# Low parts of the weights in one GpSimd subtraction each, with a wait for its end

## The reference

```
for l in range(2):
    h = rms_norm(x); z = h @ w_in            # one wide projection, split in 17 parts
    hm = mlstm(silu(conv(q, k)), v, gates)   # chunks of 128 tokens, 4 heads
    ha = dsa_attention(...)                  # 8 index heads, the 64 best keys, 8 heads
    hr = retention(rotary(rq), rotary(rk), rv)
    y = sig(g_m) * (hm @ p_m) + sig(g_a) * (ha @ p_a) + sig(g_r) * (hr @ p_r)
    x = x + y @ w_out
    x = x + (silu(h2 @ w_gate) * (h2 @ w_up)) @ w_down      # D_FF = 2816
x = rms_norm(x)
```

## Time and profile before

| | |
|---|---|
| median of 3 runs | 1605.23 us (1604.74 to 1609.58) |
| profiled execution | 1606.26 us |
| its span | 1604.4 us |
| mean granted clock of TensorE | 0.985 of full speed |
| PE busy | 1528.0 us, 95% |
| POOL busy | 1228.4 us, 77% |
| ACT busy | 714.5 us, 45% |
| DVE busy | 689.3 us, 43% |
| front (layer 0, layer 1, second block up to the experts) | 0 to about 1200 us |
| feed-forward network of layer 1 | about 782 to 960 us |

### The profile page before, as it was taken

One profiled execution on the slowest core, in us unless ns is written; L12 is line 12 of the kernel. 1 busy time (PEld: TensorE's weight loads), 2 busy tenths in 40 slices (PEclk: granted clock), 3 DMA queues, 4 the chain that ended last, 5 costly groups with the idle time before them and its releaser, 6 DMA issues.

```text
span 1604.4 us, 21618 instructions
## 1 busy us (share of the span) xinstructions
PE 1528.0 (95%) x7018; PEld 1163.9 (73%) x7018; DVE 689.3 (43%) x1306; ACT 714.5 (45%) x879; POOL 1228.4 (77%) x1185
## 2 busy tenths in 40 slices
PE   7989989999999999999999999999999899999986
PEld 5767867788887777877788887878785656646534
DVE  3995854310017977844301027456534122122215
ACT  4544543544446544543544445546341422315323
POOL 7997897988889997888888899978591633639713
PEclk9999999999999999999999999999999999999998
DMA  6754444677765553455677665645363989899990
GB/s 221 216 175 126 130 146 132 205 217 215 226 201 171 158 153 121 125 153 144 190 220 219 189 189 186 184 140 178 92 200 143 363 328 344 344 389 395 398 361 34
DMA packets 95526, 333.84 MB, mean 208 GB/s; under 512 B 11136, under 2 KB 15760, under 8 KB 94384
## 3 DMA queue, kind: packets, MB, share of 16 engines
q1 hardware_dynamic: 88240, 307.26, 58.3%
q10 hardware_dynamic: 6048, 21.22, 4.4%
q0 software_dynamic: 1152, 4.19, 0.7%
HBM read 322.12 MB, written 21.00 MB: 214 GB/s over the span
## 4 chain that ended last, share of the span: by engine, by line
POOL 49%; PE 27%; issue 19%; DMA 2%; DVE 1%; ACT 1%; POOLq 1%; ACTq 0%; DVEq 0%; SPq 0%
POOL w_lo L1890 48%; PE bank L1211 5%; PE bank L692 4%; PE bank L1279 3%; PE bank L1229 3%; PE bank L1248 3%; PE bank L696 2%; PE bank L1302 2%; PE bank L1342 1%; DMA arena<-in_experts 1%; DMA logits<-outputs_by_expert,tiny 1%; POOL w_lo L1905 1%; ACT w_hi L1455 1%; POOLq L1885 1%; PE bank L1111 0%
## 5 line engine op out<-in xcount | busy, mean ns | idle before, releaser
L1890 POOL TENSOR_TENSOR w_lo<-raw,w_hi 128x256 fp32r<-128x256 f32 (+1 forms) x1092 | 1034.2, 981 | 163.2 <-ACT w_hi L1455 161.6
L1455 ACT ACTIVATE w_hi<-raw 128x1024 fp32r<-128x1024 f32 x371 | 392.6, 1059 | 530.4 <-PE bank L696 274.9
L692 PE MATMUL bank<-w_hi,hT 128*128 128x512 f32 x2240 | 599.5, 400 | 22.3 <-DVE hT L2006 7.1
L692 PEld LDWEIGHTS bank<-w_hi,hT 128*128 128x128 f32 x2240 | 419.5, 191 | 118.2 <-issue 14.0
L696 PE MATMUL bank<-w_lo,hT 128*128 128x512 f32 x1120 | 328.1, 395 | 10.8 <-POOL w_lo L1890 10.8
L696 PEld LDWEIGHTS bank<-w_lo,hT 128*128 128x128 f32 x1120 | 211.4, 190 | 62.1 <-POOL w_lo L1890 17.1
L1905 POOL TENSOR_TENSOR w_lo<-arena,w_hi 128x1024 fp32r<-128x1024 f32 x61 | 144.5, 2390 | 125.4 <-ACT w_hi L1455 125.3
L2309 DVE SCALAR_TENSOR_TENSOR arena<-bank,tiny,arena 128x256 f32<-128x256 f32 x44 | 21.1, 483 | 169.4 <-ACT arena L1611 153.7
L1455 ACT ACTIVATE w_hi<-arena 128x1024 fp32r<-128x1024 f32 x61 | 64.0, 1057 | 57.9 <-PE bank L1211 28.4
L1014 PE MATMUL bank<-w_hi,mixT 128*128 128x512 f32 x352 | 88.0, 390 | 0.0
L692 PE MATMUL bank<-w_hi,mixT 128*128 128x512 f32 x288 | 78.8, 397 | 1.8 <-DVE xn L2283 1.8
(11 more groups left out here) (392 smaller groups left out, 1887.7 us busy)
## 6 DMA issues: line engine op xcount, KB each, us to landing
raw<-in_stream SPq DMA_DIRECT2D x357, 512.0 KB, 3.6
arena<-in_experts SPq DMA_DIRECT2D x154, 512.0 KB, 11.4
raw<-in_experts SPq DMA_DIRECT2D x38, 512.0 KB, 9.8
rows_by_expert<-in_blank ACTq DMA_DIRECT2D x56, 128.0 KB, 4.1
arena<-in_stream SPq DMA_DIRECT2D x9, 512.0 KB, 13.3
gates<-rows_by_expert SPq DMA_DIRECT2D x3, 1024.0 KB, 10.2
outputs_by_expert<-xn ACTq DMA_DIRECT2D x3, 1024.0 KB, 7.2
bias_skewed<-bias_windows SPq DMA_DIRECT2D x4, 512.0 KB, 4.9
```

What stands on the lines that cost most here:

```text
L692: pe.matmul(LIN[t][:, :], lhs[:, a, k0 + k, t * P:(t + 1) * P], w, start=(k0 + k == 0 and a == 0), stop=False)
L1455: act.activation(w_hi[:, s, :], src, ACT.Copy).then_inc(s_hi, 1)
L1890: part = nc.gpsimd.tensor_tensor(w_lo[:, i, c], raw[:, i, c], w_hi[:, i, c].bitcast(F32), ALU.subtract)
```

## The change

The constant `LOW_PARTS` and the helper with its seven loops go. One loop over all the front's quarters but the last two takes their place. In it each low part is one subtraction of 128 x 1024, which counts up `s_lo`, and behind each GpSimd waits until `s_lo` has come to this quarter's count, that is until its own subtraction has ended. `low(q)` is as it was.

```diff
-            def rounds(first, last, parts):
-                with pool.Fori(first, last) as r:
-                    for i in range(RING):
-                        pool.wait_ge(s_hi, r * RING + (i + 1))
-                        for j in range(parts):
-                            c = slice(j * QK * QC // parts, (j + 1) * QK * QC // parts)
-                            part = nc.gpsimd.tensor_tensor(w_lo[:, i, c], raw[:, i, c], w_hi[:, i, c].bitcast(F32),
-                                                           ALU.subtract)
-                        part.then_inc(s_lo, 1)
-
-            per_layer, ff = LAYER_Q // RING, 6 * (FF_GROUPS - 1) // RING
-            for l in range(LAYERS):
-                rounds(l * per_layer, (l + 1) * per_layer - ff, LOW_PARTS)
-                rounds((l + 1) * per_layer - ff, (l + 1) * per_layer - 2, 1)
-                rounds((l + 1) * per_layer - 2, (l + 1) * per_layer, LOW_PARTS)
-            rounds(LAYERS * per_layer, FRONT_Q // RING, LOW_PARTS)
+            with pool.Fori(0, FRONT_Q // RING) as r:
+                for i in range(RING):
+                    pool.wait_ge(s_hi, r * RING + (i + 1))
+                    nc.gpsimd.tensor_tensor(w_lo[:, i, :], raw[:, i, :], w_hi[:, i, :].bitcast(F32), ALU.subtract).then_inc(s_lo, 1)
+                    pool.wait_ge(s_lo, r * RING + (i + 1))
```

More of the change, by code:

```diff
@@ L38 @@
 RING = 3
-LOW_PARTS = 4
 BIG = 1e30
```

## The result

The changed kernel took 1647.0 us (1646.1 to 1650.3, 4 runs), the kernel before 1606.0 us beside it: a ratio of 1.0252, 95% interval 1.0232 to 1.0273. It is 41 us slower, where +20 was forecast: the sign was right, the size half of what came. The profiled execution took 1646.05 us, 39.8 us more than that of before, and those 39.8 us are what follows takes apart.

A forecast was written before the change was run, and what follows sets the result against it. TensorE was taken to bound; 28 us for two layers and 5 for the second block made +33, less 13 for w_lo: +20, a median of 1625 us. The range was 1596 to 1652 us, the likeliest case 1611 to 1640.

The forecast's parts named there:

- The gain: TensorE's waits for w_lo at L696: 13 of 14.9 us gone, so -13 us (ends 0 and -15).
- The own wait: GpSimd's wait behind each subtraction for its end: 0.2 us each, hidden by TensorE's 2.72 us, so 0.
- The mechanism: GpSimd locks shared ports for a whole instruction; VectorE operations pay up to 2.1 us, against 0.5 beside quarter parts.
- Place 1: Norms of the small projections, 502.0 to 530.5 us: 34 waiting VectorE operations, 1.1 us each; +5.5 us a layer.
- the ring's help: When TensorE stops, ScalarE and GpSimd get at most two to three pieces ahead, then VectorE runs free.
- Place 2: Up to the index scores: 25 VectorE operations wait 14 us instead of 8; +6, less slack: +4 us a layer.
- Place 3: Rotated queries: 12 VectorE operations wait 13 us instead of 6; +7, less 4 of slack: +3 us a layer.
- Start of a layer: Chain of norms at a layer's start (hT of L2006, where TensorE waits already): +1.5 us a layer.
- the second block: The block after the two layers, with one convolution of twelve tiles and half the chains: +5 us (0 to 12).
- A: Rival, faster, chance 0.20: four small operations pass per piece, no place comes late, the 13 us remain; 1592 us.
- C: Rival, no change, chance 0.12: three small operations pass per piece, places 1 and 2 cost the 13 us; 1605 us.
- B: Rival, far slower, chance 0.15: one VectorE operation per piece, +11 at place 3, head norms late; +47, 1652 us.

The follow-up runs named there:

- the short hold: The changed kernel, but behind the first three quarters each subtraction covers only 256 of the 1024 columns: 1567.2 us, ratio 0.9761 to the kernel before.
- one-piece-elsewhere kernel: The kernel before, with one piece, no wait for its end, in quarters 0-5, 18-47, 72-83 and the last six of each layer: 1623.7 us, ratio 1.0088.

## Why the prediction was half right

*The gain.* Forecast 13 of 14.9 us, measured all of it: no wait for w_lo is left. The premise that those 14.9 us are all that less work of GpSimd can give back is wrong, though: the short hold gave back 39.5.

*The own wait.* Forecast 0.2 us a turn-around and nothing in the end. Measured 0.16 us, and 0.39 us at the loop's branch, inside the bounds of 0.1 and 0.47; without it the kernel is 1.4 us faster in the median, no difference that can be told. The idle time put down to it is 21.6 us in all, and none of it shows in TensorE's waits. One sign of being wrong came without its meaning: GpSimd's period in the feed-forward network of layer 1 was 2.81 us, over 2.72, but those 72 quarters took TensorE 206.8 us, against 208.4 before.

*The mechanism.* Right. VectorE's operations wait for the end of the whole piece, 2.3 us instead of 0.66, with one to three small ones in between (forecast two or three). The Trainium skill, SBUF — State Buffer, section "Who interferes with whom", describes an exclusive lock, and these rows agree with it: an operation on 128x8 that takes 0.17 us beside nothing and 2.33 us beside a piece, and ends with it, is not one that shares a bandwidth.

*Place 1.* Right in the place and near in the sum, but by errors that cancel. The 34 operations were forecast at 1.1 us each and the chain, after the ring's help, 5.5 to 6 us late. It came 3.5 us longer, 0.1 us for each, so 0.8 instead of 1.1. L2349 waits 11.2 us in two where L2361 had 2.5, 4.4 more each; 1.4 and 1.8 us of clock come on top, which the forecast did not have, and the place is 5.3 and 5.6 us longer, against 5.5.

*Place 2.* Forecast +4 a layer, measured nothing. The stop at place 1, just ahead, left VectorE 8.5 us without a piece beside it. Alone, place 2 makes 7.0 us of new waits in two layers, against 8 forecast. With 3.7 us less of w_lo that would be 3.3 us net; it costs 6.6 (3.4 to 9.8). The prediction used this effect inside place 1 and forgot that it pays for the next place.

*Place 3.* Forecast +3 a layer; L2142 waits 5.15 us each. Undersized by 2. *Start of a layer.* Forecast +1.5; measured +1.1 at layer 1 (1.2 to 2.3 us of wait for hT), nothing at layer 0.

So the three places and the starts, forecast at 28 us of new waits, came to 20.1: 8.7 at L2349, 10.3 at L2142, 1.1 at hT.

*The step that failed* is the one that put everything between 600 and 760 us at nothing, without a reason, and gave the second block 5 us: "The head norms from 625 to 664 us, which I held harmless", and an attention of which the prediction says nothing at all. Head norms and attention came to 12.7 us net and the second block to 14.7, 27.4 of the 39.8 us. In the attention the softmax and the gates are long operations, each of which meets a whole piece. Two steps of the softmax, in the groups by form of before:

```profile
L2230 DVE TENSOR_TENSOR logits<-logits,tiny 128x2048 f32<-128x2048 f32 x3 | 8.5, 2823 | 0.0
L2236 DVE TENSOR_TENSOR logits<-logits,tiny 128x2048 f32<-128x2048 f32 x3 | 7.9, 2646 | 0.0
```

And of after, 1.6 and 1.1 us longer on the mean:

```profile
L2218 DVE TENSOR_TENSOR logits<-logits,tiny 128x2048 f32<-128x2048 f32 x3 | 13.4, 4467 | 0.0
L2224 DVE TENSOR_TENSOR logits<-logits,tiny 128x2048 f32<-128x2048 f32 x3 | 11.2, 3732 | 0.0
```

New waits of TensorE for the softmax, gates and scores (L2224 +7.2, L2271 +5.3, L2274 +4.6, L2181 +2.1, L2276 +1.6, L2261 +1.5) are 22.3 us, most in the layers, some in the second block. The second block, forecast at 5, cost 14.7 net, 9.2 (5.6 to 12.5) when changed alone. New waits at hT, L2706 and L2794 are 7.4 us of it, and TensorE's longer busy time 6.7. I had judged a place by whether TensorE waited there for VectorE before. It hardly did (1.8 us at L2283, 1.6 at L2286), and VectorE was busy only 44 us of 88 in the attention. But the few long operations stand directly in front of the matmuls that need them. Before, in layer 1:

```profile
691.51 4.23 DVE L2236 TENSOR_TENSOR logits<-logits,tiny 128x1024 f32<-128x1024 f32 x2
...
696.38 1.19 PE L696 MATMUL bank<-w_lo,hT 128*128 128x512 f32 x4 [2.33 <-POOL w_lo L1890]
697.41 1.28 PE L943 MATMUL bank<-cst,logits 128*128 128x128 f32 x6
```

After:

```profile
716.84 5.60 DVE L2224 TENSOR_TENSOR logits<-logits,tiny 128x1024 f32<-128x1024 f32 x2
...
722.50 0.87 PE L942 MATMUL bank<-cst,logits 128*128 128x128 f32 x6 [3.59 <-DVE logits L2224]
```

Before, VectorE was done at 695.74 us, 1.7 us ahead of L943, and TensorE had just waited 2.33 us for w_lo. So the wait for w_lo covered the softmax: without it TensorE would have been there 0.7 us before VectorE. A gain at w_lo could not be had there in full.

*A term that was missing altogether* is TensorE's clock, 8.9 of the 39.8 us. In my sum a stop cost its own length; the rows from 546 us on show that it can also cost the matmuls behind it. TensorE's busy time for the same 7018 matmuls goes with its idle time: 1516.2 us in the short hold, 1528.0 before, 1536.9 after. Which stop brought which part of it is not shown.

As a sum: -14.9 (w_lo) + 20.1 (places and starts) + 22.3 (softmax, gates, scores) + 7.4 (second block: hT 2.7, L2706 2.4, L2794 2.3) + 8.9 (clock) = 43.8, less 3.1 us of waits for ScalarE's tile of L1552 that the other stops swallowed: 40.7, against 39.8.

*The rivals.* A was to be decided at 0.8 us for each small operation of place 1. About 0.8 us came, and A failed all the same: TensorE waited longer at place 1, as the prediction said against A, and at places that A left out. C took places 1 and 2 to cost just the gain and counted no others. B came out nearest in number, 1652, by the wrong road: it had the places of the prediction cost more, and they did not.

## What to carry to other kernels

When a change lengthens what one engine holds against another, price every place where the held engine hands something to the bound one, not those alone that show a wait already: a place with no wait may have no slack either. Count a stop of the bound engine with the clock behind it, and give the time in which the other engine runs free to the next place. A wait that a change takes away may have covered another one. And choose the size of a piece for each stretch: four parts at place 1 and two behind it, in the layers, beat both kernels.

## What the runs showed that I had not expected

- A VectorE instruction of 128x1024 lasted 10.95 us (11.26 in the one-piece-elsewhere kernel) while GpSimd worked through 12 parts in a row; the same instruction takes 1.2 to 1.9 us everywhere else in the traces. It was seen in two kernels, both times in layer 1 with TensorE at quarters 195 to 197, behind the point (quarter 192) at which their parts change from two or one to four. Of their runs a few are 11 to 14 us faster than the rest, so it probably doesn't happen each time. What sets it off stays open.
- Two parts of 128x512 cost as much at place 1 as one of 128x1024, since they hold twice as many operations for half as long.
- GpSimd's work on the low parts costs the kernel before at least 39.5 us of 1607, though TensorE waits for it 14.9 us only.
